# Modulation blocks of an adaLN decoder trunk: from a VectorE fold and one ones-product to eight TensorE products with the conditioning vector as a repeated column

## What is computed

```python
c_act = jax.nn.silu(c)
for i in range(DEPTH):
    mod = (c_act @ ada_w[i] + ada_b[i])[:, None, :]
    sh1, sc1, gt1, sh2, sc2, gt2 = jnp.split(mod, 6, axis=-1)
    h = rmsnorm(x, norm_mix_g[i]) * (1.0 + sc1) + sh1
    x = x + gt1 * mixer(h)          # GLA in layer 0, gated DeltaNet in layer 1
    h = rmsnorm(x, norm_ffn_g[i]) * (1.0 + sc2) + sh2
    x = x + gt2 * peer_ffn(h, ...)
```

## Time and profile before

| | us |
|---|---|
| median of 3 runs | 2516.63 |
| the three runs | 2508.53, 2516.63, 2524.91 |
| profiled execution, its own time | 2528.67 |
| span of its instructions | 2526.9 |

### The profile page before, as it was taken

One profiled execution on the slowest core, in us unless ns is written; L12 is line 12 of the kernel. 1 busy time (PEld: TensorE's weight loads), 2 busy tenths in 40 slices (PEclk: granted clock), 3 DMA queues, 4 the chain that ended last, 5 costly groups with the idle time before them and its releaser, 6 DMA issues. The chain is left out here.

```text
span 2526.9 us, 17536 instructions
## 1 busy us (share of the span) xinstructions
PE 1624.9 (64%) x6081; PEld 726.8 (29%) x6081; DVE 1363.7 (54%) x3102; ACT 229.3 (9%) x396; POOL 1168.4 (46%) x1070
## 2 busy tenths in 40 slices
PE   7967914554554655779799897876344644644656
PEld 4534700000000000158577694455000000100001
DVE  3467486556556554146764473564756556466441
ACT  0120100000000000013321311011000000000000
POOL 0000267776777777600020201004776676677764
PEclk9988956767767667979899899888666766776779
DMA  8635669999999999935110000645899999999997
GB/s 327 271 135 204 252 222 353 369 356 350 369 328 344 364 361 371 343 126 229 72 67 1 34 1 2 244 190 191 299 359 346 344 348 365 340 363 357 352 363 252
DMA packets 162568, 667.28 MB, mean 264 GB/s; under 512 B 21536, under 2 KB 22432, under 8 KB 154800
## 3 DMA queue, kind: packets, MB, share of 16 engines
q0 software_dynamic: 147456, 536.94, 57.5%
q1 hardware_dynamic: 15024, 129.23, 13.1%
HBM read 665.05 MB, written 1.05 MB: 264 GB/s over the span
## 5 line engine op out<-in xcount | busy, mean ns | idle before, releaser
L1658 PE MATMUL PS<-vb,z 128*32 128x512 f32 x2048 | 759.7, 867 | 421.8 <-DMA vb<-in_peer_v,idx 386.7
L1555 DVE CUSTOM_DVE_ANT_0 ub<-ub,h 128x1024 f32<-128x1024 f32 x512 | 625.7, 1225 | 583.6 <-DMA ub<-in_peer_u,idx 539.4
L1698 POOL DMA_INDIRECT vb<-in_peer_v,idx x512 | 574.7, 1122 | 255.4 <-issue 147.7
L1689 POOL DMA_INDIRECT ub<-in_peer_u,idx x512 | 538.4, 1052 | 299.5 <-issue 147.2
L1658 PEld LDWEIGHTS PS<-vb,z 128*32 128x32 f32 x2048 | 115.4, 134 | 1035.6 <-DMA vb<-in_peer_v,idx 817.8
L300 PE MATMUL PS<-hT,ring 128*128 128x256 f32 (+1 forms) x1168 | 264.6, 389 | 8.9 <-DMA ring<-in_peer_wq 7.9
L300 PEld LDWEIGHTS PS<-hT,ring 128*128 128x128 f32 (+1 forms) x1168 | 226.2, 195 | 46.0 <-DMA ring<-in_peer_wq 8.3
L1641 PE MATMUL PS<-ident,spread_i 128*128 128x128 f32 x16 | 7.2, 449 | 256.3 <-DVE spread_i L1512 209.2
L1679 POOL IOTA iota<- 128x16 f32 x2 | 0.3, 150 | 324.3 <-POOLq L408 324.3
L1078 POOL COPY ring<-g 128x512 f32<-128x512 f32 x8 | 4.8, 608 | 276.5 <-POOLq L822 161.7
L254 DVE SCALAR_TENSOR_TENSOR fold<-ring,c_act,fold 128x256 f32<-128x256 f32 x280 | 112.5, 478 | 0.0
(11 more groups left out here) (271 smaller groups left out, 1778.1 us busy)
## 6 DMA issues: line engine op xcount, KB each, us to landing
ring<-in_ada_w SPq DMA_DIRECT2D x24, 2048.0 KB, 8.7
ring<-in_peer_wq SPq DMA_DIRECT2D x8, 2048.0 KB, 11.4
ring<-in_gdn_qkv SPq DMA_DIRECT2D x8, 2048.0 KB, 8.0
ring<-in_gla_w_in SPq DMA_DIRECT2D x6, 2048.0 KB, 11.0
ub<-in_peer_u,idx POOLq DMA_INDIRECT x512
vb<-in_peer_v,idx POOLq DMA_INDIRECT x512
ring<-in_gdn_z SPq DMA_DIRECT2D x4, 2048.0 KB, 7.5
ring<-in_gdn_w_out SPq DMA_DIRECT2D x4, 2048.0 KB, 11.0
```

The costliest lines, as they stand in the source:

```text
L1555: dve.tensor_tensor_reduce(out=ub[:, n % UB, :], in0=ub[:, n % UB, :], in1=h[:, tile_of(k), :], scale=1.0, scalar=0.0, op0=ALU.mult, op1=A ...
L1658: last = pe.matmul(y[t][32 * j:32 * j + 32, e, :], z[:, k % 2, j, 28 * b:28 * b + 32], vb[:, n % VB, e * 512:(e + 1) * 512], start=False, ...
L1689: pool.indirect_dma_start(ub[:, n % UB, :], None, u_rows, off).then_inc(u_land[n % UB].sem, 16)
L1698: pool.indirect_dma_start(vb[:, n % VB, :], None, v_rows, off).then_inc(v_land[n % VB].sem, 16)
```

## The change

`fold_vector` goes, with all its calls and the signal `folded`. `fold_product` waits for the block itself, and issues eight products; the stationary operand is column `k` of `c_act`, read 128 times from the same address. `fold_all` keeps only the additions.

```diff
-        def fold_vector(dve, i, n, sums):
-
-            dve.wait_ge(landed[slot_of[i]].sem, 16 * turn_of_slot[i])
-            w, last_sum = block_at(i), [0, 0]
-            for k in range(KD):
-                for part in range(2):
-                    cols = slice(part * 256, (part + 1) * 256)
-                    acc = sums[:, n % 2, cols]
-                    if k == 0:
-                        ins = dve.tensor_scalar(acc, w[:, 0, cols], c_act[:, 0:1], None, ALU.mult)
-                    else:
-                        dve.wait_ge(v_chain.sem, last_sum[part])
-                        ins = dve.scalar_tensor_tensor(acc, w[:, k, cols], c_act[:, k:k + 1], acc, ALU.mult, ALU.add)
...
-        def fold_product(pe, n, sums=fold):
-            pe.wait_ge(folded.sem, n + 1)
+        def fold_product(pe, n, i):
+
+            wait_block(pe, i)
             if n >= 2:
                 pe.wait_ge(fold_out.sem, n - 1)
-            pe.matmul(PS[:, 6 + n % 2, :], ones[:], sums[:, n % 2, :], start=True, stop=True).then_inc(used.sem, 1)
+            w = block_at(i)
+            for k in range(KD):
+                last = pe.matmul(PS[:, 6 + n % 2, :], c_act[:, k:k + 1].to_broadcast([P, P]), w[:, k, :], start=(k == 0), stop=(k == KD - 1))
+            last.then_inc(used.sem, 1)
...
-        def fold_all(dve, plan, first, sums=fold):
-
-            due = None
+        def fold_all(dve, plan, first):
+
             for at, (kind, n) in enumerate(plan):
                 if kind == "mod":
-                    fold_vector(dve, first + at, n, sums)
-                    if due:
-                        fold_add(dve, *due)
-                    due = (first + at, n)
-            if due:
-                fold_add(dve, *due)
+                    fold_add(dve, first + at, n)
```

More of the change, by code:

```diff
@@ L147, in trunk_kernel @@
         bias_landed, gain_landed = signal("bias_landed"), signal("gain_landed")
-        folded, fold_out = signal("modulation_folded"), signal("modulation_added")
+        fold_out = signal("modulation_added")
         idx_ready, ex_ready, exp_done = signal("idx_ready"), signal("scores_less_top"), signal("scores_exp")
@@ L504, in _ @@
                         if kind == "mod":
-                            fold_product(pe, b)
+                            fold_product(pe, b, first + at)
                             continue
@@ L535, in _ @@
                         if kind == "mod":
-                            if at:
-                                fold_vector(dve, first + at, b, fold)
                             if added:
@@ L684, in _ @@
                             last.then_inc(emptied["D"].sem, 1)
-                    fold_vector(dve, consumed[0], OUT_PLAN[0][0][1], fold)
                     dve.wait_ge(rooted.sem, rooted.at(1))
@@ L972, in _ @@
                                 dve.wait_ge(bias_landed.sem, 32)
-                                fold_vector(dve, index["mod", folds[b]], folds[b], fold)
                             dve.wait_ge(proj_out.sem, proj_out.at(b + 2))
@@ L1310, in _ @@
                         if t == T - 1:
-                            fold_vector(dve, index["z", nz - 1] + 1, OUT_PLAN[1][0][1], fold)
+                            pass
                         for jj in range(2):
```

## The result

| | before | after |
|---|---|---|
| median, us | 2516.43 (4 runs) | 2627.0 (4 runs, 2621.9 to 2639.8) |
| ratio (of the means) | | 1.0446, 95% interval 1.0393 to 1.05 |
| profiled execution, its own time | 2528.67 | 2621.90 |
| its span | 2526.9 | 2620.1 |

The kernel became slower by 110.6 us in the medians; 104.2 was forecast (2621 with the level of before, inside 2605 to 2638). In a second series the same changed kernel was 106.3 us slower (2638.81 against 2532.55), ratio 1.0417, 1.0364 to 1.047.

The account below looks back on a forecast made before the run. PE was taken to bound the dense stages holding all 20 modulation blocks. Stage terms 34.2 + 21.6 + 6.2 + 12.0 + 24.0 + 6.2 = 104.2 us on 2516.63 gave 2621 us, range 2605 to 2638.

Parts of the forecast that it names:

- The price of a block: All 20 modulation blocks: eight products cost PE 6.86 us, replacing one of 0.86, so 6.0 us added each.
- The open term: New products: loading a stationary operand from one repeated column takes 190 ns, hidden under the row before, at no cost.
- GLA's output: GLA's output projection, 4 blocks: +21.6 us, with the full clock coming about 5.0 us after the first products.
- The three credits: GLA output: residual half added during block 9; query projections: 3.97 us load wait gone, 1.8 us from full clock.
- The term that was mis-sized: GLA's input projection, 6 blocks: 36.0 us of products less 1.8 us credit, net +34.2 us.
- the two late products: GLA's input projection: two products delayed by the fold, PEld idle 0.94 and 1.34 us; 1.8 us come back.
- The gather stages: rigid shift: PEER's gather stages, without modulation blocks, start later but keep their length: 0 us change.
- (a): Rival, new products: repeated-column loads are slow; at 0.76 us each, 106 us more, 2727 us; chance 5%.
- (b): Rival, query projections: PE's load wait or slow clock stays, 2 x 5.8 us credit lost, 2632 us; chance 6%.
- (c): Rival, every block: PE waits for VectorE's fold, so 124.5 us is swapped for 120, ending at 2512; chance 2%.
- (d): Rival, product stream: rows run faster than now, at half the price, about 2575 us; chance 2%.
- (e): Rival, longer dense stretches lose the full clock: products cost 6.9 us more each, up to 2758; chance 2%.

Follow-up runs that it names:

- the copied tile: Changed kernel with the stationary operand read from a tile holding each column copied 128 times: 2635.14 us, ratio to the kernel before 1.0402.
- reproduced without the products: Kernel before, folded on VectorE, second query-projection modulation block behind the third query block and folded after `routing(0)`: 2462.39 us against 2475.83, ratio 0.9945.
- The second pair of profiles: Kernel before and changed kernel, both unedited, profiled again in the second series; medians 2532.55 and 2638.81 us, ratio 1.0417.
- when I moved a block myself: Kernel before, folded on VectorE, second query-projection modulation block moved behind the second query block: 2532.10 us against 2519.46, ratio 1.0062.
- the first series: Kernel before and changed kernel, 4 runs each, the main result: medians 2516.43 and 2627.0 us, ratio 1.0446.
- kernels of the fourth: Fourth series: kernels folding all or part of their blocks on VectorE; one, with only the query projections' four blocks on TensorE, took 2478.78 us.

## Why the prediction was right

**The bound.** PE ends last in every stage that holds modulation blocks. Shown: 20 blocks doubled cost 134.9 us of 137.2, and VectorE's 121 us less bought nothing beyond the credits. One reading was too narrow: the 0.5 us that the fold held PE is the idle time of the product rows; the load rows of the same line (L264) stood 4.5 us for the fold, five times, by the same trace. The sum took the two of GLA's input projection among them, and the rest is too small to matter.

**The price of a block,** 6.86 us, was read from four blocks of the kernel before; it measured 6.87. The open term, the load of a repeated column, was taken at 190 ns and measured 190; the copied tile confirms that it is free beside distinct columns.

**The stages.** GLA's output, both query projections, DeltaNet's input and output came within 0.7 us of their terms. The three credits behind them (residual half moved under the last block, load wait, full clock) are each seen in the rows above, and the last two were reproduced without the products. That GLA's output came within 0.1 us has some luck in it: the term was worked out for a clock that rises some 5 us into the stage, and both profiles of the changed kernel had it so; where the clock was up from the start, the stage took 64.2 us with the products and 43.5 with the fold, a difference of 20.7.

**The term that was mis-sized** is GLA's input projection: +38.2 for +34.2. Of the 4.0 us, 3.0 are the first block at 17.05 us where the profile before had 14.05, longer at half clock; kernels with the fold in this stage scatter as far (16.97), and with GLA's blocks alone on TensorE the stage gave +35.1. The second pair of profiles gives +36.7 with a first block 1.4 us longer, so 0.9 to 1.1 us remain each time. The larger part is the credit for the two late products. I took it from the idle time of the load rows, 1.8 us; from start to start PE lost only 1.26: the projection blocks before them took 14.01 and 14.41 where the others take 13.73, and the two products 0.96 and 1.06 for 0.86. In the second profile of the kernel before only the last one was late, and PE lost 0.87. In the first pair another 0.3 us is ahead of the first block, where the second set of transposes took 1.97 us for 1.71.

**"The gather stages: rigid shift"** holds for the first (-0.7) and failed for the second in this pair of profiles (-14.3). Since folded kernels show short ones too, I count most of it as scatter between executions and series; that was argued from the set of profiles and not tried by itself, and a part of a few us that belongs to the change stays possible. What sets the length of a gather stage from one execution to the next stays open. Of the 6.4 us between the forecast and the medians' difference, 3.6 are in the dense stages; the other 2.8 are within the noise, and how long the gather stages were in the runs without a profile is not known.

**The rivals.** (a) slow loads: out, 190 ns. What stood against it, that every load in the trace takes 190 ns whatever its source, was too broad: L1128 and L1162, also 128x128, have medians of 141 and 140 ns. (b) the wait stays: out, it was 0; it did come in another form when I moved a block myself. (c) the fold sets the pace: out, the fold had held PE for a few us and not 6 a block. (d) a faster stream: out, 6.87 us a block. The 131 ns of the Trainium skill, "TensorE: Matmul & The Clock Gate" (Back-to-back issue gap), did not show for full-width products: 429 ns a row, or 214 a pass if a row is two passes, as the prediction took it. Only products in different column groups ran closer. (e) the clock falls: out. The mean of 0.97 is below the 1.00 that was named as the sign, but the added products did not bring it down: it is the slow start of the first block, and from 70 to 180 us the clock is 1.00.

## What to carry to other kernels

A vector times a matrix is one row of result, but a product with a repeated stationary column costs TensorE as much as one with 128 distinct columns (429 ns a trace row in both); where another engine has room and TensorE sets the pace, fold there and leave TensorE the one sum. If it must be on TensorE, spread the contraction over four column groups and add up once: 2.8 us a block for 6.9. Before a block is moved in a plan, follow every in-order queue that it passes, not only the one it is on: here the slack of 27 us on VectorE was cut by an exponential in ScalarE's queue. And before two profiles are compared to a microsecond, look at the granted clock at the head of each stage behind a gap: it alone moved single stages by 1.5 to 3 us here, in either kernel.

## What the runs showed that I had not expected

Four column groups of float32 products, each with its own stationary column and its own partitions of one PSUM bank, ran at 0.116 us a row (1.86 / 16) against 0.429, with loads of 32 columns at 110 ns. And the gather stages differ more between the series than within one: the last one took 769 us in the kernel before in the first series, and 739 and 726 in kernels of the fourth with the same bytes. DMA moved up to 402 GB/s in a slice there and at most 373 in the first. The median of the kernel before fell as well, from 2516 to 2476.

GLA's output projection has a clock that rises early or late, and nothing between was seen: the stage took 45.0 or 43.5 us in the kernels that fold its blocks, and 66.7 or 64.2 in the changed kernel and the one with the copied column. With the fold the whole hardly changes by it, since the mixer's core ahead is 1.3 us longer where it rises early. Why one execution has it early and another late was not tried.
